# One layer of a hybrid diffusion block: filter taps as two fp32r passes, gate weights in three slots, value transfers on two queues, another order in the opening

## The reference

```python
hx = modulate(rmsnorm(x, norm1_g), sh1, sc1)          # shift and scale from silu(c) @ w_mod
zx = hx @ w_in + b_in                                 # 5120 columns
# Hyena filters: MLP over positions, then taps = h @ w3, times a decay
h = sin(freq * (feats @ w1 + b1)); h = sin(freq * (h @ w2 + b2))     # (1024, 64)
filt = (h @ w3).reshape(L, 2, 2, 512) * decay         # w3: (64, 2048)
y = x1 * long_conv(v, filt[:, 0, 0], filt[:, 1, 0]);  y = x2 * long_conv(y, filt[:, 0, 1], filt[:, 1, 1])
na = neighbourhood_attention(q, k, v, kc, vc, rpb)    # 8 heads of 64, local keys and 256 context keys
mix = (sigmoid(z[g_hy]) * (y @ w_branch_hy) + sigmoid(z[g_na]) * (na @ w_branch_na)) @ w_out
x = x + g1 * mix
x = x + g2 * expert_choice_moe(modulate(rmsnorm(x, norm2_g), sh2, sc2))   # 16 experts, 128 tokens each
out = rmsnorm(x, final_g)
```

## Time and profile before

| | us |
|---|---|
| median of 3 runs (2685.49 to 2688.57) | 2688.33 |
| profiled execution | 2691.22 |
| its span, first to last instruction | 2689.1 |
| PE busy in the span | 2552.8 |
| DVE busy | 2121.5 |
| ACT busy | 1469.7 |
| mean granted TensorE clock, share of full speed | 0.977 |

### The profile page before, as it was taken

The page is one execution under the profiler, slowest core; times in us unless marked ns, Lnnn a source line. Parts: engine busy times, 40 slices in busy tenths (PEclk is TensorE's granted clock), DMA queues, the critical chain, the costliest instruction groups (busy, mean ns, idle before and its releaser), DMA issues.

```text
span 2689.1 us, 32278 instructions
## 1 busy us (share of the span) xinstructions
PE 2552.8 (95%) x12649; PEld 2130.0 (79%) x12649; DVE 2121.5 (79%) x1976; ACT 1469.7 (55%) x1249; POOL 145.1 (5%) x151
## 2 busy tenths in 40 slices
PE   6999979999999999399999999999999999999997
PEld 3777869878878878378888888888888888888885
DVE  5675237667889655689888888988888888888887
ACT  4522236531121212177777777777777777777774
POOL 0011000011111000000000000000000000000000
PEclk9999989999999999699999999999999999999998
DMA  7499674465577633399999999999999999999994
GB/s 273 161 323 305 220 220 108 136 196 149 151 211 224 221 110 117 156 378 364 380 396 370 365 399 383 363 381 394 371 364 400 381 364 383 393 371 365 396 379 172
DMA packets 197988, 792.84 MB, mean 295 GB/s; under 512 B 17807, under 2 KB 65271, under 8 KB 127888
## 3 DMA queue, kind: packets, MB, share of 16 engines
q1 hardware_dynamic: 165508, 701.08, 68.8%
q0 software_dynamic: 29488, 86.01, 10.5%
q10 hardware_dynamic: 2846, 3.74, 0.5%
HBM read 719.18 MB, written 67.39 MB: 293 GB/s over the span
## 4 chain that ended last, share of the span: by engine, by line
PE 52%; issue 2%; ACT 2%; DVE 2%; DVEq 0%; ACTq 0%
PE moe_ps_gate L2308 18%; PE moe_ps_y L2298 16%; PE moe_ps_up L2308 16%; PE moe_ps_h L2279 2%; ACT moe_w_hi L2354 1%; DVE moe_w_lo L2406 1%; PE moe_ps_x L2269 1%; DVE raw L2478 0%; ACT moe_xt_hi L2347 0%; DVE moe_h L2429 0%; PE moe_ps_x L2313 0%; ACT moe_sl L2367 0%; DVE raw L2465 0%; PE moe_ps_gate L2337 0%; PE moe_ps_gate L2339 0%
## 5 line engine op out<-in xcount | busy, mean ns | idle before, releaser
L2406 DVE TENSOR_TENSOR moe_w_lo<-raw,moe_w_hi 128x2048 fp32r<-128x2048 f32 x528 | 1207.4, 2290 | 156.4 <-ACT moe_w_hi L2354 156.4
L2354 ACT ACTIVATE moe_w_hi<-raw 128x2048 fp32r<-128x2048 f32 x528 | 1010.6, 1919 | 378.8 <-PE moe_ps_gate L2308 125.9
L2308 PE MATMUL moe_ps_up<-moe_w_hi,moe_xt_hi 128*128 128x512 f32 (+1 forms) x768 | 292.3, 381 | 0.0
L2308 PE MATMUL moe_ps_gate<-moe_w_hi,moe_xt_hi 128*128 128x512 f32 (+1 forms) x768 | 288.1, 375 | 1.0 <-DVE moe_xt_lo L2397 1.0
L2308 PE MATMUL moe_ps_up<-moe_w_hi,moe_xt_lo 128*128 128x512 f32 (+1 forms) x768 | 286.4, 373 | 0.0
L2308 PE MATMUL moe_ps_up<-moe_w_lo,moe_xt_hi 128*128 128x512 f32 (+1 forms) x768 | 285.9, 372 | 0.0
L2308 PE MATMUL moe_ps_gate<-moe_w_hi,moe_xt_lo 128*128 128x512 f32 (+1 forms) x768 | 285.7, 372 | 0.0
L2308 PE MATMUL moe_ps_gate<-moe_w_lo,moe_xt_hi 128*128 128x512 f32 (+1 forms) x768 | 285.1, 371 | 0.0
L2298 PE MATMUL moe_ps_y<-moe_w_hi,moe_ht_hi 128*128 128x512 f32 x704 | 218.6, 392 | 1.9 <-DVE moe_ht_lo L2434 1.9
L2298 PE MATMUL moe_ps_y<-moe_w_lo,moe_ht_hi 128*128 128x512 f32 x704 | 217.0, 389 | 0.0
L2298 PE MATMUL moe_ps_y<-moe_w_hi,moe_ht_lo 128*128 128x512 f32 x704 | 217.0, 389 | 0.0
(11 more groups left out here) (296 smaller groups left out, 3724.3 us busy)
## 6 DMA issues: line engine op xcount, KB each, us to landing
raw<-in_w_moe SPq DMA_DIRECT2D x528, 1024.0 KB, 7.2
hyena_g_parts<-gw_d POOLq DMA_DIRECT2D x64, 512.0 KB, 4.7
proj_w_mod<-in_w_mod SPq DMA_DIRECT2D x32, 512.0 KB, 7.1
gw_d<-proj_g_parts POOLq DMA_DIRECT2D x16, 1024.0 KB, 7.5
w_in<-in_w_in SPq DMA_DIRECT2D x12, 1024.0 KB, 8.2
attn_table<-in_na_table SPq DMA_DIRECT2D x16, 576.0 KB, 5.5
norm_w_mod<-in_w_mod SPq DMA_DIRECT2D x16, 512.0 KB, 11.0
proj_g_raw<-in_w_in SPq DMA_DIRECT2D x16, 512.0 KB, 10.0
```

The costliest lines, as they stand in the source:

```text
L2308: mm = pe.matmul(ps, hp[:, e % 2, k, :], wp[:, r, :], start=(k == 0 and x == 0), stop=(k == KD - 1 and x == 2))
L2354: act.activation(w_hi[:, g % PARTS], raw[:, g % RAW], ACT.Copy).then_inc(hi_ready, 1)
L2406: dve.tensor_tensor(w_lo[:, g % PARTS], raw[:, g % RAW], w_hi[:, g % PARTS].bitcast(F32), ALU.subtract).then_inc(lo_ready, 1)
```

## The change

- Taps: h and w3 are loaded raw, each twice, into rows 0 to 63 and 64 to 127. h2 becomes the high part of h in both halves, w3 the high part in rows 0 to 63 and the low part in rows 64 to 127, h_low the low part of h in 64 rows. A product of taps is then one fp32r matmul over 128 rows and one over 64. The parts are made in the attention stage, by twelve ACT copies (`tap_unit`) and six DVE subtractions (`tap_low_unit`) at listed steps; the two memsets go. The raw tiles lie where h2 and w3 lie, and the loads move from the end of the attention stage's loads to behind table 1.
- Gate weights: three slots in place of four.
- Values: ACT copies tiles 0, 1, 2 and 4, SP 3, 5 and 6 (before it waits for its stores of h), and 7 as before.
- Opening: the MLP's second layer after chunk 0; three `turn` groups of x after chunk 2, ahead of chunk 3; 6 and 10 transposes of the identity into an unused buffer around the sixteen small ones; DVE's second sine argument ahead of row 1, and row 2 behind `split(0)`.

```diff
@@ norm_and_project @@
+ACT_SPREADS, SP_SPREADS = (0, 1, 2, 4), (3, 5, 6)
...
+        WARM_ROW, WARM_FILL = 6, 10
...
+                for t in SP_SPREADS:
+                    sp.wait_ge(evacuated, V_AT + 2 + t + 1)
+                    spread_values(sp, keep, t)
                 sp.wait_ge(keep["kept"], KEPT_H)
...
-                    if n == 1:
+                    if n == 0:
                         pe.wait_ge(mlp_sin, 1)
                         mlp(w2[:], hidden)
+                    if n == NC - 2:
+                        pe.wait_ge(mlp_arg, 2)
+                        for x in range(3):
+                            turn(x)
+                for _ in range(WARM_ROW):
+                    pe.transpose(ps_room[:, 0, 0:P], ident[:], ident[:])
                 pe.wait_ge(mod_row_ready, NC)
...
-                pe.wait_ge(mlp_arg, 2)
-                turn(0)
-                turn(1)
+                for _ in range(WARM_FILL):
+                    pe.transpose(ps_room[:, 0, 0:P], ident[:], ident[:])
                 pe.wait_ge(lo_ready, 1)
                 for n in range(CTX_FILL):
-                    if n + 2 < CTX_FILL:
+                    if n and n + 2 < CTX_FILL:
                         turn(n + 2)
...
-                for t in range(TT - 1):
+                for t in ACT_SPREADS:
                     act.wait_ge(evacuated, V_AT + 2 + t + 1)
                     spread_values(act, keep, t)
...
                 sine_argument(0)
                 early_row(0)
+                sine_argument(1)
                 early_row(1)
-                sine_argument(1)
                 scales(0)
...
-                early_row(2)
...
                 split(0)
+                early_row(2)
                 early_row(3)
@@ attend @@
+TAPS_IN = 16 * 4
+TAP_SLOTS = [(0, 13), (0, 14), (0, 15), (1, 5), (1, 6), (1, 7), (1, 13), (1, 14), (1, 15), (2, 5), (2, 6), (2, 7)]
+TAP_LOW_SLOTS = [TAP_SLOTS[n] for n in (1, 2, 3, 5, 7, 9)]
...
                 load_table(sp, a, keep, 1)
+                for rows in (slice(0, FC), slice(FC, 2 * FC)):
+                    sp.dma_start(h2_raw[rows], a["hidden_d"]).then_inc(keep["hyena_in"], 16)
+                    sp.dma_start(w3_raw[rows], a["filt_w3"]).then_inc(keep["hyena_in"], 16)
                 for g in range(2, HEADS):
...
-                for dst, name in ((keep["h2"][0:FC, :], "hidden_d"), (keep["w3"][0:FC, :], "filt_w3"),
-                                  (keep["dft"][:], "dft"), (keep["idft"][:], "idft")):
+                sp.wait_ge(keep["hyena_in"], TAPS_IN)
+                for dst, name in ((keep["dft"][:], "dft"), (keep["idft"][:], "idft")):
...
+                    if (j, s) in TAP_SLOTS:
+                        tap_unit(TAP_SLOTS.index((j, s)))
+
+                def tap_unit(x):
+                    if x < 2:
+                        cols = slice(512 * x, 512 * x + 512)
+                        if x == 0:
+                            act.wait_ge(keep["hyena_in"], TAPS_IN)
+                            act.wait_ge(v_in[1], spread(TT - 1))
+                        act.activation(h_low[0:FC, cols], h2_raw[0:FC, cols], ACT.Copy).then_inc(tap_high, 1)
+                    elif x < 10:
+                        c = x // 2 - 1
+                        cols = slice(512 * c, 512 * c + 512)
+                        if x % 2 == 0:
+                            if c:
+                                act.wait_ge(tap_low, 2 + c)
+                            act.activation(part[FC:P].bitcast(F32R), w3_raw[FC:P, cols], ACT.Copy
+                                           ).then_inc(tap_high, 1)
+                        else:
+                            act.activation(w3[0:FC, cols], w3_raw[0:FC, cols], ACT.Copy)
+                    else:
+                        cols = slice(512 * (x - 10), 512 * (x - 10) + 512)
+                        act.wait_ge(tap_low, x - 9)
+                        act.activation(h2[:, cols], h2_raw[:, cols], ACT.Copy)
...
+                    if (j, s) in TAP_LOW_SLOTS:
+                        tap_low_unit(TAP_LOW_SLOTS.index((j, s)))
+
+                def tap_low_unit(x):
+                    dve.wait_ge(tap_high, x + 1)
+                    if x < 2:
+                        cols = slice(512 * x, 512 * x + 512)
+                        ins = dve.tensor_tensor(h_low[0:FC, cols], h2_raw[0:FC, cols], h_low[0:FC, cols].bitcast(F32),
+                                                ALU.subtract)
+                    else:
+                        cols = slice(512 * (x - 2), 512 * (x - 2) + 512)
+                        ins = dve.tensor_tensor(w3[FC:P, cols], w3_raw[FC:P, cols], part[FC:P], ALU.subtract)
+                    ins.then_inc(tap_low, 1)
...
-                        if j == 0 and s == 1:
-                            dve.memset(keep["w3"][FC:P, :], 0.0)
-                            dve.memset(keep["h2"][FC:P, :], 0.0)
@@ hyena @@
+        G_SLOTS, G_K = 3, KD // 2
-        G_SLOTS, G_K = 4, KD // 2
...
-                pe.wait_ge(consts_in, 4 * 16)
+                pe.wait_ge(consts_in, TAPS_IN + 2 * 16)
...
-                        mm = pe.matmul(ps_tap[:, x % 2, s * HALF_C:(s + 1) * HALF_C], h2[:, ph * P:(ph + 1) * P],
-                                       w3[:, at:at + HALF_C], start=True, stop=True)
+                        to, rows = ps_tap[:, x % 2, s * HALF_C:(s + 1) * HALF_C], slice(ph * P, (ph + 1) * P)
+                        pe.matmul(to, h2[:, rows], w3[:, at:at + HALF_C], start=True, stop=False)
+                        mm = pe.matmul(to, h_low[0:FC, rows], w3[0:FC, at:at + HALF_C], start=False, stop=True)
                     mm.then_inc(tap_done, 1)
```

More of the change, by code:

```diff
@@ L207, in norm_and_project @@
             ps_early = f.psum("ps_mod", [P, 2, 512])
-            f.psum("ps_room", [P, 2, 512])
+            ps_room = f.psum("ps_room", [P, 2, 512])
             ps_x = f.psum("ps_x", [P, 3, 512])
@@ L909, in attend @@
         keep["table"].append(m.sb("table1", [P, 3 * TABLE]))
+        m.sb("room_l", [P, 8208])
+        h_low = keep["h_low"] = m.sb("h_low", [P, T], F32R)
+        part = m.sb("tap_part", [P, 512])
+        h2, w3, h2_raw, w3_raw = (keep[n] for n in ("h2", "w3", "h2_raw", "w3_raw"))
+        tap_high, tap_low = sems("tap_high"), sems("tap_low")
         q_two, k_hi, k_lo, table, v_band = (keep[n] for n in ("q_two", "k_hi", "k_lo", "table", "v_band"))
@@ L1190, in hyena @@
         turned = m.sb("turned", [P, 2, 2, HALF_C])
+        G_SLOTS, G_K = 3, KD // 2
+        g_parts = m.sb("g_parts", [P, G_SLOTS, 2, G_K, P], F32R)
         u_tok = m.sb("u_tok", [P, 4, HALF_C])
+        m.sb("room_l", [P, 48 + T])
+        h_low = keep["h_low"]
         gate = m.sb("gate", [P, 2, T])
-        G_SLOTS, G_K = 4, KD // 2
-        g_parts = m.sb("g_parts", [P, G_SLOTS, 2, G_K, P], F32R)
         h_parts = m.sb("h_parts", [P, 2, KD, SPAN], F32R)
@@ L2527, in program @@
                 keep["merge"] = merge_places(nc, sems)
+                with ExitStack() as places:
+                    n = Maker(nc, places)
+                    keep["w3_raw"] = n.sb("w3_raw", [P, 4 * HY])
+                    keep["h2_raw"] = n.sb("h2_raw", [P, T])
                 n = Maker(nc, convolving)
-                keep["w3"] = n.sb("w3", [P, 4 * HY])
-                keep["h2"] = n.sb("h2", [P, T])
+                keep["w3"] = n.sb("w3", [P, 4 * HY], F32R)
+                keep["h2"] = n.sb("h2", [P, T], F32R)
                 keep["dft"] = n.sb("dft", [P, PH, 3, P])
```

## The result

| | before | after |
|---|---|---|
| median of 4 runs each, us | 2687.59 (2685.49 to 2688.57) | 2706.31 (2704.09 to 2708.99) |
| profiled execution, its span | 2691.22, 2689.1 | 2706.98, 2704.9 |
| PE busy | 2552.8 | 2572.9 |
| mean granted clock | 0.977 | 0.976 |

What follows compares the result with a forecast made beforehand. It took PE as carrying the chain from 1144 us, delayed one for one by what precedes. Opening -4.7, values -3.3, attention +0.5, taps -8.1, slots +4.4 sum to -11.2 us: 2677.1 us, range 2669 to 2685, chance 0.60.

Steps and rivals of the forecast that it cites:

- Taps, -8.1: Hyena stage: a tap unit falls from 0.86 to 0.47 us, counting only where PE is the bound; sum -8.1 us.
- the second pass has 64 rows only, but columns set the time: Taps: the 64-row matmuls were taken at 0.12 us each like the others, so 0.47 us per unit.
- one more pass for each unit: Taps: a split needing an extra pass would cost 32 x 0.24 = 7.7 us; set aside because of the diff.
- Attention, +0.5: Attention steps: added tap copies, subtractions and loads are nearly hidden; +0.5 us, bounds 0 and +4.
- issued 2.5 us ahead of head 2's loads, which are needed 15 us later: Attention: the four tap loads on SP, 1.5 MB and some 4 us, were expected to do no harm there.
- upper bound of +4: Attention: the cost if a third of the 18 added copies and subtractions were laid bare.
- Slots, +4.4: Gate weights: three slots cost +0.7 us in the bursts of three gates and 3.7 in the last eight gates.
- Rival (c): Gate weights: three slots become the pace of every burst, +33 us in place of +4.4, 2705.7 us; chance 0.06.
- Values, -3.3: Value transfers: split between ACT and SP, attention starts near 370.7 us; -3.3 us, bounds -1.5 and -5.5.
- row of share 0.41: Value transfers: DMA engines' share was 0.41 in 362 to 372, taken to mean issuing, not moving, is the bound.
- Opening, -4.7: Opening: first fill 3.0 us earlier, 1.7 more by the reciprocal; -4.7 us, bounds -2 and -6.
- 16 filler transposes shorten the pauses: Opening: fillers (6 and 10) around the small transposes; -0.9 us if the clock stays at 2.4 GHz.

Runs made afterwards that it cites:

- e1: Kernel after with the second tap pass over all 128 rows, rows 64 to 127 of h_low set to zero: 2689.0 us.
- e5: Kernel after with the two passes of a unit's second phase swapped, the 64-row pass first: 2698.9 us.
- e4: Kernel after with the four tap loads issued behind head 2's q and k instead of ahead of them: 2698.6 us.
- e3: Kernel before with three slots for gate weights in place of four, nothing else changed: 2694.1 us, ratio 1.0023.
- e8: Kernel before with the value transfers on two queues alone: 2686.2 us, ratio 0.9993.
- e7: Kernel before with the new order of the opening alone: 2686.4 us, ratio 0.9993.
- e9: Kernel after with full-row taps, tap loads behind head 2's, and gate room cut into six quarter slots: 2681.2 us.
- e10: As e9, with 22 filler transposes in place of 10 ahead of the first latent matmuls: 2678.8 us.
- e11: As e3, with two of attention's three row loads for the merge moved behind the last segment gates: 2689.9 us, ratio 1.0013.

## Why the prediction was wrong

- **Taps, -8.1; they took 9.5.** The step that failed is "the second pass has 64 rows only, but columns set the time". It took the pitch of the earlier trace rows, where both matmuls have 128 rows, for a pair of unequal rows. With alternating heights the matmuls stand 0.31 apart in place of 0.12, because each change of height costs 0.2 us (e1, e5), and a unit costs 1.25 us for the 0.47 of the sum. With full rows the rest of the step was right: -0.39 from unit to unit (2.59 to 2.20), and -6.5 us for the stage, of which my count of which units matter promised -8.1. I gave the taps no bounds on the far side of nothing; the one remark of such a size, "one more pass for each unit", I had ruled out by the diff.
- **Attention, +0.5; it took 5.3.** The compute part was right (+0.3, e4). The loads were mis-placed: "issued 2.5 us ahead of head 2's loads, which are needed 15 us later" compared the need with the issue, and not with the landing. Head 2's k landed after 8.0 us at the median and up to 9.6 in before; with 1.5 MB ahead, up to 14.1. The wait then was 2.75 us, and the clock made it 5. The upper bound of +4 was for another cause and too low.
- **Slots, +4.4; alone they cost +5.4 (e3),** in the place named. But the path was another: 0.0 in the bursts for +0.7, and in the last gates 2.4 of waiting for the 3.7, plus some 2 of a clock that my sum didn't have. Rival (c) didn't occur.
- **Values, -3.3; -2.1 (e8).** The path was right: attention starts 15.0 to 15.1 us after tile 3's landing wherever that falls. The size hangs on this landing, which in e8 came 1.8 us later than I had it; the -2.1 itself is not clear of nothing. Of the rule weighed there (the Trainium skill, "DMA: Bandwidth & Descriptors", Issuing engines are not separate DMA queues), that several issuing engines save only issue time, usually little, the first half agrees with the row of share 0.41 and the second doesn't fit: here that time came to about 2 us in the mean of the profiles (16.2 against 18.2), since 56 issues of 0.612 us stood in a row.
- **Opening, -4.7; about -2 (e7), not clear of nothing either.** With the clock at 1.00 the values do end about 4.5 us earlier than before's (355.2 against 359.7), but at 0.50, the usual case, only 1.3 to 2.4. "16 filler transposes shorten the pauses" didn't keep the clock up in five of eight profiles; what decides between the two stays open. The pause of 4.5 us, which the MLP's move made longer (2.67 before), slowed chunk 2 in after (its first twelve matmuls took 5.25 us, in e1 4.44).
- **The forecast at 0.60 and "slower" at 0.07** rested on a slower rival of one mechanism alone (c). Two new causes, each outside the sum, came to 5 us and 17 us.

## What to carry to other kernels

When a matmul pass needs only half the rows, and its neighbours have all 128, pad it with zeros: more work was faster here, because the weight loads then ran ahead. Where it can't be padded, put the passes of equal height side by side. When loads are moved ahead on a queue, compare what stands behind them with its landing time plus theirs, not with its issue. A long wait of PE can have a second price in the clock behind it, here 2.0 us behind e3's 4.31 and 4.0 behind e9's 3.3; waits of up to 1.85 us in the same place didn't have it, so a burst is worth splitting even if no byte is saved.

## What the runs showed of the hardware

- fp32r matmuls of 256 columns with 128 rows each stand 0.12 us apart. Where one of 64 rows follows one of 128, or the reverse, the weight load doesn't run ahead, and the change costs 0.2 us: from unit to unit 2.98 us with four changes (after), 2.59 with two (e5), 2.20 with none (e1). Two matmuls of 64 rows one behind the other pay nothing (e5).
- From fp32 to fp32r at equal height nothing is paid. The first fp32r matmul only starts early, 0.03 us behind the last fp32 record (556.51 and 556.54 in e1) and 0.31 ahead of the next; the whole unit costs 0.47, four times 0.12.
- In the last gates the granted clock went from 2.4 to 1.2 GHz behind waits of PE of 2.6 us (e10), 3.3 (e9), 4.1 (after) and 4.3 (e3), and stayed up over 1.85 in before and 1.27 in e11. In the opening it fell in five of eight executions of the same code, in three of them early in a pause of 1.54 us and in two ahead of one of 1.1, and in three it stayed up over 1.54.
